# Token rows of the second expert stage: picked on chip by one-hot products in place of gathers from DRAM

## The chip, the cores and the metric

The kernel runs on one core of a Trainium2 chip. The metric is the time of one launch on the device, in microseconds (us); lower is better. TensorE is called PE (its weight loads PEld), VectorE DVE, ScalarE ACT, GpSimd POOL and SyncE SP, as in the profile.

## What is computed

The program is a stack of layers over 256 token rows of 1024 numbers, all in float32: a first block (two mixers, two feed-forward layers) and a second block of two layers, each ending in a mixture of experts. This is the mixture, cut to what matters here:

```
g_idx = top 1 of 4 groups;  top_i = top 2 of the 8 experts in it;  gate = softmax(top_v) * g_val
order = argsort(e_flat); row_tok = the token of each sorted slot; xb = x_pad[row_tok]
def expert_block(xblk, e): return (silu(xblk @ w1[e]) * (xblk @ w3[e])) @ w2[e]
out[row_tok] += yb * row_gate
```

There are 32 experts; w1 and w3 are 1024 x 512 and w2 is 512 x 1024, so one expert's weights are three matrices of 2 MB. The first expert stage routes 512 rows (256 tokens and 256 context rows), the second 256. A token goes to two experts, so in the second stage an expert gets 16 rows on average.

## The kernel before, in words

The class `Experts` holds both stages; `nt` is the number of 128-row token tiles, 4 in the first stage and 2 in the second. The text below is about the second (`nt == 2`).

The experts are taken in 16 pairs. A pair has 128 slots, 64 (`CAP`) for each of its two experts; a token's slot in its expert is its rank among the tokens that chose the expert. Rows past 64 go to an overflow loop that runs only if there are any; in this profile it does not run. The normed and modulated token rows stand in SBUF in `XM`, two tiles of 128 rows (columns 0 to 2047 of the arena Z), and ACT's copies of them are also written to DRAM, to `xm_dram`, by POOL (L2478).

Pair 0 gets its rows by a one-hot product (`pe_first`, L2042): DVE builds `SEL`, for each token and slot a 1 where the token's place equals the slot, and PE multiplies `XM` with it, which gives the rows already turned (the model dimension on the partitions). Every other pair c gets them by an indirect DMA that POOL issues (L2483): slot r reads the row of `xm_dram` that `LIST[r, c]` names, and a slot without a token has an index past the bound and reads nothing. It lands in `XG[:, c % 2]`. `XG` is the same memory as `XM[:, 0:2]`, and `c % 2` is one of two buffers: so the first gather waits until pair 0 is turned, and gather c for `turn1.{c-2}`. PE then turns the 128 x 1024 rows with 8 transposes (`pe_turn`, L2031), and ACT and DVE copy the two banks to `XT[c % 2]` (L2230, L2289).

The order on PE in a pair c is written out: w1 product (`pe_hidden` q=0, L2058, 32 matmuls), w3 product (q=1, 32 more), `pe_turn(c + 1)`, the combine of pair c-1 (L2091: 4 matmuls that spread the outputs back over tokens, which DVE adds to X, L2411), 4 transposes of the hidden rows (L2068), w2 product (L2078, 32 matmuls). For c = 0 the turn of pair 1 stands at the end of the pair. On DVE a pair is: product of the two hidden halves (L2416), copy of the turned rows (L2289), 4 adds, `PICK` (L2428), two products with the gates (L2404), which wait for the w2 product.

The weights of a pair are 6 loads of 2 MB (L1995), 96 in all, from SP in order; load n goes to slot n % 8 of eight 2 MB areas and waits until the product that used load n-8 is done. Loads 6c and 6c+1 are w1 of pair c, 6c+2 and 6c+3 w3, 6c+4 and 6c+5 w2. Nothing but these slots orders the loads against PE.

Of the kernel before, what the change touches and what calls it, by code (L numbers as in the profile page):

```python
# [22 lines left out]
P = 128  # L23
# [154 lines left out]
def build_program(nc, a, out, table, PARAM_AT, stop=None):  # L178

    ctx = ExitStack()  # L180
    with ctx:
# [36 lines left out]
        def upto(who, key):  # L218
            return table.get((who, key), 1)
# [1698 lines left out]
        class Experts:  # L1918
            def __init__(self, layer, nt, before, following):
                self.l, self.nt, self.before, self.following = layer, nt, before, following  # L1920
                L = f"moe{layer}"
                self.L = L
                s = lambda n: sem(f"{L}_{n}")
                self.w_loaded = [s(f"weights{i}_loaded") for i in range(MSLOTS)]
                self.xm_written = s("inputs_written")
                self.rows_in = [s(f"rows_in{b}") for b in range(2)]
                self.units = [(t, n) for g in range(nt // 2) for n in range(2) for t in (2 * g, 2 * g + 1)]
                self.free = "yx" if nt == 2 else "yc"
                self.selected = s("over_selection_steps")
                self.picked, self.xa = s("over_rows_picked"), s("over_rows_copied")  # L1930
                self.t1, self.m1, self.t2, self.m2 = s("over_rows_turned"), s("over_hidden_ready"), s("over_hidden_turned"), s("over_block_ready")
                self.xt, self.sl, self.y = s("over_rows_t_copied"), s("over_silu_done"), s("over_block_copied")
                self.h, self.g = s("over_hidden_copied"), s("over_gated_done")
                self.slots_turned, self.slots_of = s("over_slots_turned"), s("over_slots_copied")
                self.block, self.made, self.added = s("over_outputs_copied"), s("over_sums_ready"), s("over_sums_added")
                self.o_loaded, self.o_rows = s("over_loaded"), s("over_inputs_loaded")
                self.w = [a[f"w{j}_2"][layer] for j in (1, 3, 2)]
                self.rb = RB[:, 0:2 * nt].rearrange("p (t k) -> p t k", t=nt)

                self.owners = sorted((n for n in before_moe[layer]), key=[n for n, _ in stream].index)  # L1940
                self.slots = [slots[slot_of[n]] for n in self.owners[:4]] + [Z[:, 4096:8192], Z[:, 8192:12288], slots[slot_of[self.owners[4]]], HTF]
                self.o_slots = [self.slots[i] for i in (4, 5, 7)]
                self.OXM = self.slots[6].rearrange("p (t n) -> p t n", t=4)
                self.OS = Z[:, 0:CAP * nt].rearrange("p (t r) -> p t r", t=nt)
                self.ohit = Z[:, 256:256 + 2 * CAP * nt].rearrange("p (t k r) -> p t k r", t=nt, k=2)
                R = XSF[:, 0:1024]
                self.LG = R[:, 0:36 * nt].rearrange("p (t n) -> p t n", t=nt)
                self.OH = R[:, 144:144 + 64 * nt].rearrange("p (t k e) -> p t k e", t=nt, k=2)
                self.CT = R[:, 400:400 + 32 * (nt + 1)].rearrange("p (t e) -> p t e", t=nt + 1)
                self.CNT, self.EX, self.END, self.STA = [R[:, 656 + 32 * i:688 + 32 * i] for i in range(4)]  # L1950
                self.OHW = YW[1][:, 0:64 * nt].rearrange("p (t k e) -> p t k e", t=nt, k=2)
                self.FIRST = R[:, 560:560 + 2 * nt].rearrange("p (t h) -> p t h", t=nt)
                self.SEL = XSF[:, 1280:1280 + 2 * CAP * nt].rearrange("p (t h r) -> p t h r", t=nt, h=2)
                self.TM = SM[:, 256:256 + 64 * nt].rearrange("p (t k e) -> p t k e", t=nt, k=2)
                self.M8 = R[:, 784:784 + 8 * nt].rearrange("p (t n) -> p t n", t=nt)
                self.IF = R[:, 816:816 + 8 * nt].rearrange("p (t n) -> p t n", t=nt)
                self.OHT = XSF[:, 1024:1024 + 64 * nt].rearrange("p (t k e) -> p t k e", t=nt, k=2)
                self.HR = YW[0][:, 0:2 * CAP * nt].rearrange("p (t k r) -> p t k r", t=nt, k=2)
                q = lambda i, n: SM[:, 512 + 16 * i:512 + 16 * i + n]
                self.gm, self.gv, self.g0, self.tmp = [q(i, nt) for i in range(4)]  # L1960
                self.GO = q(4, 4 * nt).rearrange("p (t g) -> p t g", t=nt)
                self.G2 = q(5, 4 * nt).rearrange("p (t g) -> p t g", t=nt)
                self.GW = q(6, 2 * nt).rearrange("p (t k) -> p t k", t=nt)
                self.rk, self.qq, self.st, self.sl_, self.ov = [q(i, 2 * nt).rearrange("p (t k) -> p t k", t=nt) for i in range(7, 12)]
                self.EC = SM[0:1, 256:768].rearrange("p (j e) -> p j e", j=16)
                self.EO = R[0:1, 848:868]
# [30 lines left out]
            def sp(self, sp, tiles):  # L1997
# [8 lines left out]
                sp.wait_ge(sems["pe"], upto("pe", f"{self.L}.out1.{PAIRS - 1}"))  # L2006
                n = sp.value_load(OVF[0:1, 16:17], min_val=0, max_val=15)
                with sp.If(n > 0):
                    sp.dma_start(self.OXM[:, 0:self.nt, :], xm_dram[0:P * self.nt, :].rearrange("(t p) d -> p t d", p=P)).then_inc(self.o_rows, 16)
                    with sp.Fori(0, n) as j:  # L2010
                        sp.wait_ge(self.y, j + 1)
                        e = sp.value_load(OVF[0:1, bass.ds(j, 1)], min_val=0, max_val=NE - 1)
                        for k in range(3):
                            src = self.w[k][bass.ds(e, 1)].rearrange("a (p k) n -> p (a k n)", p=P)
                            sp.dma_start(self.o_slots[k], src).then_inc(self.o_loaded, 16)
# [6 lines left out]

            def pe_turn(self, te, c):
                pe, p, L, b = te.eng, te.p, self.L, c % 2
                pe.wait_ge(self.rows_in[b], 16 * (c // 2) + 16 * b)
                if c >= 1:
                    pe.wait_ge(sems["act"], upto("act", f"{L}.xt0.{c - 1}"))
                    pe.wait_ge(sems["dve"], upto("dve", f"{L}.xt1.{c - 1}"))
                for hf in range(2):
                    for j in range(4):  # L2030
                        m = pe.transpose(PS[:, hf, P * j:P * j + P], XG[:, b, 512 * hf + P * j:512 * hf + P * j + P], ident)  # L2031
                    p.step(m, f"{L}.turn{hf}.{c}")


# [252 lines left out]
            def dve_xt(self, dv, p, c):  # L2287
                dv.wait_ge(sems["pe"], upto("pe", f"{self.L}.turn1.{c}"))
                p.step(dv.tensor_copy(XT[c % 2][1], PS[:, 1, :].rearrange("p (j r) -> p j r", j=4)), f"{self.L}.xt1.{c}")  # L2289

            def dve(self, dv, p):
                L, nt, l = self.L, self.nt, self.l

                def do(instr, *key):
                    p.step(instr, *key)
                    p.settle()
# [34 lines left out]
                for t in range(nt):  # L2331
# [14 lines left out]
                do(dv.scalar_tensor_tensor(out=self.FIRST, in0=rank[:, :, 0:2], scalar=1.0, in1=self.CT[:, 0:nt, 0:2], op0=ALU.add, op1=ALU.mult))  # L2346
                p.step(dv.tensor_tensor(self.SEL, four(self.FIRST, CAP), cst("iota")[:, 1:CAP + 1].unsqueeze(1).unsqueeze(1).to_broadcast([P, nt, 2, CAP]),
                                        ALU.is_equal), f"{L}.sel")
                do(dv.tensor_tensor(self.TM, self.OH, per_choice(rank.unsqueeze(2)), ALU.mult))
                do(dv.tensor_reduce(self.rk, self.TM, AXX, ALU.add))  # L2350
                p.step(dv.tensor_tensor(self.HR, four(self.rk, CAP), row_of(cst("iota"), CAP), ALU.is_equal), f"{L}.hot")
                p.step(dv.tensor_copy(self.CNT, PS[:, 4, 32 * nt:32 * nt + 32]), f"{L}.rk")
                self.dve_xt(dv, p, 0)
                dv.wait_ge(sems["pe"], upto("pe", f"{L}.lists"))
                do(dv.tensor_scalar(LIST[:, 0:PAIRS], PS[:, 5, 0:PAIRS], float(NO_TOKEN), None, ALU.add), f"{L}.list")
                for t in range(nt):
                    p.step(dv.tensor_scalar(TOKEN_IN[:, :, t], PS[:, 5, 0:PAIRS], float(NO_TOKEN - P * t), None, ALU.add))
# [55 lines left out]
                for c in range(PAIRS):  # L2413
# [11 lines left out]
                    else:  # L2425
                        for i in range(2 * nt):
                            add(c - 1, i)
                    p.step(dv.tensor_tensor(PICK[:, 0:nt, :], cst("iota").unsqueeze(1).to_broadcast([P, nt, P]),  # L2428
                                            TOKEN_IN[:, c, 0:nt].unsqueeze(2).to_broadcast([P, nt, P]), ALU.is_equal), f"{L}.pick.{c}")
                    if c == 1:  # L2430
                        n_over = dv.value_load(OVF[0:1, 16:17], min_val=0, max_val=15)
                    for n in range(2):
# [3 lines left out]
                    if late:  # L2436
                        self.dve_xt(dv, p, 1)
                with dv.If(n_over > 0):
                    with dv.Fori(0, n_over) as j:
                        dv.wait_ge(self.selected, 6 * j + 1)  # L2440
                        dv.tensor_tensor(self.ohit, four(self.rb, CAP), row_of(cst("iota"), CAP), ALU.is_equal).then_inc(self.selected, 1)
# [31 lines left out]
            def pool(self, po):  # L2473
# [4 lines left out]
                    po.dma_start(xm_dram[P * t:P * t + P, :], XM[:, t, :]).then_inc(self.xm_written, 16)  # L2478
                po.wait_ge(sems["dve"], upto("dve", f"{L}.list"))
                po.wait_ge(self.xm_written, 16 * self.nt)  # L2480
                for c in range(1, PAIRS):
                    po.wait_ge(sems["pe"], upto("pe", f"{L}.turn1.{max(c - 2, 0)}"))
                    po.indirect_dma_start(XG[:, c % 2, :], None, xm_dram[:, :], bass.IndirectOffsetOnAxis(ap=LIST[:, c:c + 1], axis=0),  # L2483
                                          bounds_check=4 * P - 1, oob_is_err=False).then_inc(self.rows_in[c % 2], 16)
# [160 lines left out]
```

## Time and profile before

| | |
|---|---|
| median of 3 runs | 2274.24 us (2269.87 to 2276.2) |
| the profiled execution, its own time | 2264.46 us |
| its span | 2262.6 us |
| PE busy | 2153.8 us (95%) |
| DVE, ACT, POOL busy | 882.4 (39%), 314.9 (14%), 46.6 us (2%) |
| moved by DMA | 612.00 MB, mean 270 GB/s |
| mean granted PE clock | 0.984 of full speed |

The span runs from the first to the last instruction of the core. Busy shares are means over the whole span. The second expert stage fills the last fifth: PE starts pair 0 at 1788.7 us, the last weights arrive near 2241 us, and the last add is at 2258.3 us. A granted clock of 1.00 is 2.4 GHz and 0.50 is 1.2 GHz.

### The profile page before, as it was taken

To read this page: it belongs to the slowest core of one execution; us is meant where nothing else is said; L and a number is where in the kernel's file an instruction comes from. 1 tells how busy PE (TensorE), PEld (TensorE's weight loads), DVE (VectorE), ACT (ScalarE), POOL (GpSimd) and SP (SyncE) were. 2 spreads that over 40 slices of the span, in tenths; PEclk is the share of its full clock that TensorE was granted. 3 is DMA by queue.
4 is the path that set the end of the run, shared out by engine and by line. 5 is a ranking of instruction groups with operands and counts; after the bars stand their busy time and mean duration, and the time that the engine had idled before them with its cause. 6 is when DMAs were issued, how large, how long until landed. Compare 5 with 4: busy or idle time off the path is not lost.

```text
span 2262.6 us, 21849 instructions
## 1 busy us (share of the span) xinstructions
PE 2153.8 (95%) x8991; PEld 1129.6 (50%) x8991; DVE 882.4 (39%) x1623; ACT 314.9 (14%) x686; POOL 46.6 (2%) x62
## 2 busy tenths in 40 slices
PE   7999999998999999999899999999899899989898
PEld 4557766455577764444633333333345543333333
DVE  3336665326365654022432333323575422121122
ACT  2221001215310003000100000000134100000000
POOL 0000000000000000000100000000000000000000
PEclk9999999998999999999899999999999899999999
DMA  9347766350276675121899999999320899999995
GB/s 356 119 149 260 260 238 232 124 186 34 81 261 226 243 269 186 40 74 38 349 424 418 413 411 418 414 413 394 130 76 1 350 427 425 427 428 426 427 427 243
DMA packets 142532, 612.00 MB, mean 270 GB/s; under 512 B 15320, under 2 KB 66200, under 8 KB 117728
## 3 DMA queue, kind: packets, MB, share of 16 engines
q1 hardware_dynamic: 135328, 596.07, 66.7%
q0 software_dynamic: 7008, 14.40, 1.8%
q8 instruction: 74, 1.21, 0.2%
q14 instruction: 26, 0.21, 0.0%
q10 hardware_dynamic: 96, 0.10, 0.0%
HBM read 616.07 MB, written 4.33 MB: 274 GB/s over the span
## 4 chain that ended last, share of the span: by engine, by line
PE 91%; ACT 3%; DVE 3%; issue 2%; DMA 1%; SPq 0%; ACTq 0%; DVEq 0%
PE psum L2058 19%; PE psum L494 14%; PE psum L981 13%; PE psum L2078 10%; PE psum L2091 8%; PE psum L956 6%; PE psum L1559 4%; PE psum L534 3%; PE psum L2031 1%; PE psum L969 1%; PE psum L607 1%; PE psum L2068 1%; PE psum L480 1%; ACT consts L2253 1%; PE psum L1695 1%
## 5 line engine op out<-in xcount | busy, mean ns | idle before, releaser
L981 PE MATMUL psum<-normed_t,ring 128*128 128x256 f32 x1408 | 305.5, 379 | 0.0
L981 PEld LDWEIGHTS psum<-normed_t,ring 128*128 128x128 f32 x1408 | 267.5, 190 | 40.6 <-issue 4.3
L494 PE MATMUL psum<-ring,normed_t 128*128 128x512 f32 (+1 forms) x672 | 267.0, 557 | 9.9 <-DVE small L447 2.5
L886 DVE SCALAR_TENSOR_TENSOR arena<-ring,silu_c,arena 128x1024 f32<-128x1024 f32 x168 | 204.5, 1278 | 0.0
L494 PEld LDWEIGHTS psum<-ring,normed_t 128*128 128x128 f32 x672 | 124.3, 200 | 142.5 <-issue 140.9
L2078 PE MATMUL psum<-ring,consts 128*64 128x512 f32 x640 | 169.8, 594 | 21.5 <-ACT consts L2253 19.7
L2416 DVE TENSOR_TENSOR scaled<-scaled,psum 128x512 f32<-128x512 f32 x32 | 22.0, 687 | 426.8 <-PE psum L2058 426.8
L2091 PE MATMUL psum<-consts 128*128 128x512 f32 x384 | 186.1, 606 | 1.1 <-DVE small L447 0.2
L2058 PE MATMUL psum<-ring,arena 128*64 128x512 f32 x640 | 173.4, 609 | 9.7 <-issue 9.2
L2058 PE MATMUL psum<-ring,consts 128*64 128x512 f32 x640 | 168.4, 593 | 6.8 <-issue 6.8
L2411 DVE TENSOR_TENSOR resid<-resid,psum 128x512 f32<-128x512 f32 x192 | 131.8, 687 | 48.2 <-PE psum L2091 48.2
L2404 DVE SCALAR_TENSOR_TENSOR consts<-psum,consts,rows_bcast 128x512 f32<-128x512 f32 x96 | 69.3, 749 | 208.0 <-PE psum L2078 208.0
L956 PE MATMUL psum<-ring,arena 128*128 128x512 f32 x288 | 126.3, 596 | 0.0
L2058 PEld LDWEIGHTS psum<-ring,arena 128*64 128x64 f32 x640 | 62.3, 141 | 113.0 <-issue 113.0
L2078 PEld LDWEIGHTS psum<-ring,consts 128*64 128x64 f32 x640 | 59.3, 137 | 111.4 <-issue 111.4
L2091 PEld LDWEIGHTS psum<-consts 128*128 128x128 f32 x384 | 59.9, 188 | 107.0 <-DVE resid L2411 86.9
L2058 PEld LDWEIGHTS psum<-ring,consts 128*64 128x64 f32 x640 | 59.1, 137 | 107.9 <-issue 107.3
L956 PEld LDWEIGHTS psum<-ring,arena 128*128 128x128 f32 x288 | 53.9, 190 | 72.5 <-issue 72.0
L1559 PE MATMUL psum<-normed_t,ring 128*128 128x512 f32 x192 | 82.6, 592 | 0.0
L2248 ACT ACTIVATE scaled<-psum 128x512 f32<-128x512 f32 x32 | 19.1, 597 | 439.0 <-PE psum L2058 439.0
L1041 DVE SCALAR_TENSOR_TENSOR arena<-psum,params,arena 128x255 f32<-128x255 f32 x44 | 21.2, 481 | 150.7 <-ACT arena L1012 150.7
L1012 ACT ACTIVATE arena<-psum,params 128x256 f32<-128x256 f32 x44 | 24.9, 566 | 381.1 <-PE psum L981 381.1
(398 smaller groups left out, 2217.0 us busy)
## 6 DMA issues: line engine op xcount, KB each, us to landing
ring<-in_w SPq DMA_DIRECT2D x120, 2048.0 KB, 18.0
arena<-in_w SPq DMA_DIRECT2D x48, 2048.0 KB, 19.6
ring<-in_w_mod SPq DMA_DIRECT2D x24, 2048.0 KB, 8.1
normed_t<-in_w SPq DMA_DIRECT2D x24, 2048.0 KB, 21.0
ring<-in_ffn_w_up SPq DMA_DIRECT2D x44, 1024.0 KB, 9.4
ring<-in_ffn_w_down SPq DMA_DIRECT2D x10, 2048.0 KB, 9.4
ring<-in_ab_w_in SPq DMA_DIRECT2D x6, 2048.0 KB, 17.3
ring<-in_ple_w_gate SPq DMA_DIRECT2D x4, 2048.0 KB, 9.5
```

The costliest lines, as they stand in the source:

```text
L494: m = te.eng.matmul(PS[:, bank, 0:n], src[:, k0 + k, P * t:P * t + P], w[:, k, :], start=(k == 0), stop=(k == kc - 1))
L534: m = pe.matmul(PS[:, bank, :], HT[:, k, P * t:P * t + P], w[:, k, :], start=(k == 0), stop=(k == KC - 1))
L886: ins = dv.scalar_tensor_tensor(out=acc, in0=w, scalar=sc, in1=acc, op0=ALU.mult, op1=ALU.add)
L956: m = pe.matmul(PS[:, 4 + 2 * n + t, :], GT[:, c, P * t:P * t + P], w[:, cc, 512 * n:512 * n + 512], start=(c == 0), stop=(c == FC - 1))
L981: m = pe.matmul(PS[:, b, 256 * hf:256 * hf + 256], w[:, hf, k, P * cc:P * cc + P], HT[:, k, 0:T], start=(k == 0), stop=(k == KC - 1))
L1012: p.step(ac.activation(AC[:, c % 4, :], PS[:, c % 3, 0:256], ACT.Identity, bias=f_cb[i][:, c:c + 1], scale=f_cw[i][2][:, c:c + 1]), f"ffn{ ...
L1559: m = pe.matmul(PS[:, b0 + c, :], w[:, k, P * c:P * c + P], HT[:, k, :], start=(k == 0), stop=(k == KC - 1))
L2058: m = pe.matmul(PS[64 * h:64 * h + 64, 2 + q, :], XT[c % 2][k // 4][:, k % 4, 64 * h:64 * h + 64], w[h][:, k, :], start=k == 0, stop=k == ...
L2078: m = pe.matmul(PS[64 * h:64 * h + 64, 6 + n, :], HGT[:, j, 64 * h:64 * h + 64], w[h][:, j, 512 * n:512 * n + 512], start=j == 0, stop=j == 3)
L2091: m = pe.matmul(PS[:, 4 + i % 2, :], PICK[:, t, :], YW[t // 2][:, 512 * n:512 * n + 512], start=True, stop=True)
L2404: p.step(dv.scalar_tensor_tensor(out=YW[kind][:, cols], in0=PS[:, 6 + n, :], scalar=SLOT_GATE[:, c:c + 1], in1=GB[:, kind, cols], op0=ALU. ...
L2411: p.step(dv.tensor_tensor(xr, xr, PS[:, 4 + i % 2, :], ALU.add), f"{L}.add{i}.{c}", *keys)
```

## The change

For `nt == 2` the gathers are not issued. DVE keeps a table `PLACE` of each token's slot in each of the 32 experts (0 where the token did not choose it), and for each pair builds `SELS[c % 2]`, the one-hot matrix of its two experts, two pairs ahead. `pe_turn` multiplies `XM` with it, as pair 0 did, in place of the transposes. `XM` is then never overwritten. `SELS` and `PLACE` lie in a part of the arena that the second stage does not use. The rows are still written to `xm_dram`, for the overflow; the waits for that write are added there. The first stage (`nt == 4`) is as before.

```diff
@@ Experts.__init__
+                self.picks = nt == 2
+                self.PLACE = Z[:, 2560:2624].rearrange("p (t e) -> p t e", t=2)
+                self.SELS = [Z[:, o:o + 256].rearrange("p (t h r) -> p t h r", t=2, h=2) for o in (2048, 2304)]
@@ sp, in the overflow (and the same in dve)
+                    sp.wait_ge(self.xm_written, 16 * self.nt)
@@ pe_turn
-                pe.wait_ge(self.rows_in[b], 16 * (c // 2) + 16 * b)
+                if self.picks:
+                    pe.wait_ge(sems["dve"], upto("dve", f"{L}.sel.{c}"))
+                else:
+                    pe.wait_ge(self.rows_in[b], 16 * (c // 2) + 16 * b)
...
                 for hf in range(2):
                     for j in range(4):
-                        m = pe.transpose(PS[:, hf, P * j:P * j + P], XG[:, b, 512 * hf + P * j:512 * hf + P * j + P], ident)
+                        cols = slice(512 * hf + P * j, 512 * hf + P * j + P)
+                        if self.picks:
+                            for t in range(2):
+                                m = pe.matmul(PS[:, hf, P * j:P * j + P], XM[:, t, cols], self.SELS[b][:, t].rearrange("p h r -> p (h r)"),
+                                              start=t == 0, stop=t == 1)
+                        else:
+                            m = pe.transpose(PS[:, hf, P * j:P * j + P], XG[:, b, cols], ident)
@@ new
+            def dve_sel(self, dv, p, c):
+                if c > 2:
+                    dv.wait_ge(sems["pe"], upto("pe", f"{self.L}.turn1.{c - 2}"))
+                p.step(dv.tensor_tensor(self.SELS[c % 2], self.PLACE[:, :, 2 * c:2 * c + 2].unsqueeze(3).to_broadcast([P, 2, 2, CAP]),
+                                        cst("iota")[:, 1:CAP + 1].unsqueeze(1).unsqueeze(1).to_broadcast([P, 2, 2, CAP]), ALU.is_equal),
+                       f"{self.L}.sel.{c}")
@@ dve, routing: after SEL
+                if self.picks:
+                    p.step(dv.scalar_tensor_tensor(out=self.PLACE, in0=rank, scalar=1.0, in1=self.CT[:, 0:nt, :], op0=ALU.add, op1=ALU.mult))
@@ dve, routing: before LIST
+                if self.picks:
+                    self.dve_sel(dv, p, 1)
+                    self.dve_sel(dv, p, 2)
@@ dve, in each pair after PICK
+                    if self.picks and 1 <= c < PAIRS - 2:
+                        self.dve_sel(dv, p, c + 2)
@@ pool
-                for c in range(1, PAIRS):
+                for c in range(1, 1 if self.picks else PAIRS):
```

## Rows read from the trace of the kernel before

**Rows 1.** Second expert stage by stretches: us, each engine busy, PEclk, DMA share, GB/s
```profile
1790.00:2262.00 472.00, 429.38 (x1860) 171.71 (x1856) 100.36 (x173) 29.77 (x51) 14.95 (x15) 0.98 0.96 405
```
**Rows 2.** DMA queues from 1800 to 2235 us: packets, MB, share of 16 engines
```profile
q1 hardware_dynamic: 12557, 182.87, 98.9%
q0 software_dynamic: 2160, 1.97, 1.3%
```
**Rows 3.** Chain that ended last, 1740 us to the end: start us, us, what
```profile
1840.82 13.73 PE psum L2058 x64
...
1867.97 13.73 PE psum L2058 x64
...
1902.51 7.09 PE psum L2058 x32
...
1932.56 8.78 PE psum L2058 x32
...
2022.63 7.09 PE psum L2058 x32
2029.71 1.02 PE psum L2031 x8
...
2043.13 6.87 PE psum L2058 x32
2050.00 2.65 issue
2052.65 8.51 PE psum L2058 x32
...
2114.25 8.43 PE psum L2058 x32
...
2174.27 8.78 PE psum L2058 x32
...
2203.64 7.09 PE psum L2058 x32
...
2231.01 1.98 issue
2232.99 8.78 PE psum L2058 x32
2241.78 1.92 PE psum L2091 x4
```
**Rows 4.** Waits from 1790 us on: who, for whom, us in total, times, longest
```profile
PE psum L2058 <- issue: 23.3, 13, 2.7
```
**Rows 5.** PE timeline, a turn in this stage: start us, us, instructions
```profile
1827.33 1.09 PE L2031 MATMUL psum<-consts,arena 128*128 128x128 f32 x8
1828.26 1.88 PE L2091 MATMUL psum<-consts 128*128 128x512 f32 x4
```
**Rows 6.** PE timeline, the one-hot product of pair 0 in the first expert stage
```profile
1099.94 7.38 PE L2042 MATMUL psum<-scaled,arena 128*128 128x128 f32 x64 [1.07 <-DVE scaled L2347]
1107.25 0.94 PE L2157 MATMUL psum<-scaled,consts 128*64 128x16 f32 x26
```
**Rows 7.** Groups from 1780 us on: busy us, mean ns, idle before and releaser
```profile
L2404 DVE SCALAR_TENSOR_TENSOR consts<-psum,consts,rows_bcast 128x512 f32<-128x512 f32 x32 | 24.1, 752 | 111.6 <-PE psum L2078 111.6
L2428 DVE TENSOR_TENSOR consts<-consts 128x256 f32<-128x256 f32 x16 | 6.7, 420 | 0.0
```
**Rows 8.** DMA queue of the gathers in one pair, 2052.65 to 2082.67 us
```profile
q0 software_dynamic: 144, 0.11, 1.1%
```
**Rows 9.** Stretches as the weight stream ends, and as another load ends at 1609 us
```profile
2230.00:2242.00 12.00, 10.02 (x39) 3.58 (x36) 0.18 (x1) 0.60 (x1) 0.00 (x0) 0.86 0.49 208
2230.00:2231.00 1.00, 1.00 (x6) 0.13 (x2) 0.00 (x0) 0.00 (x0) 0.00 (x0) 1.00 0.96 410
2240.00:2241.00 1.00, 1.00 (x8) 0.38 (x5) 0.00 (x0) 0.00 (x0) 0.00 (x0) 1.00 0.12 49
1608.00:1609.00 1.00, 0.79 (x3) 0.30 (x2) 0.96 (x4) 0.00 (x0) 0.00 (x0) 1.00 1.02 389
1609.00:1610.00 1.00, 0.64 (x3) 0.24 (x3) 1.00 (x3) 0.00 (x0) 0.00 (x0) 1.00 0.23 84
```

More of the change, by code:

```diff
@@ L2438, in dve @@
                 with dv.If(n_over > 0):
+                    dv.wait_ge(self.xm_written, 16 * nt)
                     with dv.Fori(0, n_over) as j:
```

## The prediction

> **What bounds the kernel now.** Over the whole span PE is 95% busy, and the chain of waits is nearly all PE. For this change that is the wrong view, so I read the second expert stage alone. The busy time by stretches says that there the DMA engines are 96% busy at 405 GB/s on average [rows 1], and between 1800 and 2235 us nothing is free: the weight queue has 98.9% of the 16 engines and POOL's queue 1.3% more [rows 2]. The chain of waits then shows when that binds. Early pairs run at PE's pace: the w1 product starts at 1840.82 and the next at 1867.97, 27.15 us apart. From 1902.51 on, the chain has pieces called "issue" in front of the w3 product (L2058), as the 2.65 us before 2052.65 [rows 3]. Such a piece is a wait that the profile can't name; here it is the wait for the second w3 load of the pair, n = 6c + 3, since the w1 and w2 products that need the loads on either side start late enough. There are 13 of them, 23.3 us in all [rows 4]. The w3 products of pairs 4 and 15 start at 1902.51 and 2232.99: 330.48 us for 11 pairs, 30.04 us a pair, against 27.15 of PE's own work. So PE is ahead, the weight stream is the bound from pair 4 on, and the stream ends the kernel: when load 93 lands (2232.99), PE has the last w3 product, the combine, w2 and the last combine left, and that tail is fixed.
>
> After some of these waits the w3 product takes longer than 7.09 us: 8.78, 8.51, 8.43, 8.78 and, in the last pair, 8.78 [rows 3]. In the last one the granted clock is 0.86 over 2230 to 2242 us [rows 9]: part of it ran at 1.2 GHz after the idle. The four before the last sum to 1.69 + 1.42 + 1.34 + 1.69 = 6.14 us, which is wait in another form.
>
> **Part 1: what PE gets more.** A turn is 8 transposes now. From the start of one (1827.33) to the start of the combine (1828.26) are 0.93 us, 116 ns each [rows 5]. It becomes 16 matmuls of 128 x 128 with 128 columns, accumulated in pairs. The trace has just this form in `pe_first` of the first stage, at full clock: 64 of them start in 1107.25 - 1099.94 = 7.31 us, 114 ns each [rows 6]. 16 x 114 = 1.83 us, so a turn costs 0.90 us more, 0.92 with the transposes' own price; 15 turns make 13.8 us. I take 0.92: the upper end is a turn at the low clock, twice 1.83 less 0.93, +2.7 us, the lower end nothing, if matmuls of two tiles overlapped as transposes don't. The copies by ACT and DVE behind the turn, and the combine with its adds, shift with it.
>
> All but one turn stand behind a w3 product and ahead of the next wait for weights, so this work falls into waits that PE has anyway, as long as there are enough. The stock is the 23.3 us of waits and the 6.14 of slow products, 29.4 us up to the start of the last w3 product. Without them PE would start it at 2232.99 - 29.4 = 2203.5; with 13.8 more, at 2217.4. What is left of the cover is 15.6 us before the stream moves at all.
>
> A rule that speaks against the change is in the Trainium skill, page FP8 and Floating Point Precision, section TensorE Precision Notes: a true float32 product takes four passes through the array. The row disagrees with what it would cost: 128 columns four times at 2.4 GHz would be 213 ns, and [rows 6] has 114, no more than a transpose. By the rule 16 x 213 ns less 0.93 would be 2.48 us a turn; the sum goes by the row.
>
> **Part 2: what DVE gets more.** One `SELS` a pair, of the form of PICK: 128 x 256, 420 ns [rows 7]. It stands between PICK and the products with the gates, and these wait for the w2 product: 111.6 us of idle before 32 of them, 3.5 us each [rows 7]. So 0.42 us is hidden eight times over; without that cover it would delay the next w2 product's bank and cost up to 0.42 x 13 = 5.5 us. `PLACE` and the first two `SELS` (some 1.1 us) lie in the routing; PE is by then in the one-hot product and the 13.8 us of the first two hidden products, and DVE is next needed after those. PE's new wait for `sel.{c}` was served a pair earlier: nothing. The waits for `xm_written` stand in an overflow that does not run: nothing.
>
> **Part 3: what the DMA engines lose.** This is where the time is. 15 gathers go. POOL's queue takes 1.3% of 435 us, 5.7 us of each engine on the mean [rows 2]; small, since slots without a token read nothing (0.11 MB in one pair, not the 0.52 MB of 128 rows) [rows 8]. This is the least that the stream can gain, 0.38 us a pair.
>
> But a load is there only when the last of its 16 engines is done, and the engines are not equally late. Pairs that still have a gather ahead of their loads are 30.02 us apart (2022.63 to 2052.65); after the last gather the spacing is 29.37 and 29.35 (2174.27, 2203.64, 2232.99) [rows 3]. That is 0.66 us a gather, where the mean share of such a pair is 1.1% of 30.02, 0.33 us [rows 8]. And the end of the stream shows it: another load on this core stops within a microsecond (share 1.02, then 0.23), while the weight stream fades from 0.96 at 2230 to 0.12 at 2240 [rows 9]. Some engines are ten microseconds ahead of others, and the last one sets when load 93 is complete.
>
> The Trainium skill gives a reason (DMA: Bandwidth & Descriptors, The descriptor swizzle): an engine owns fixed partitions, the first owning 0 to 3 and 32 to 35. Used slots are the first 16 or so of each 64, so half of the engines would carry all rows, twice the mean. The 0.66 against 0.33 agrees, and with a reason beside the rows I give the case where only the mean is saved a smaller chance than the two spacings alone would leave it.
>
> How early is load 93 then? Two ways:
> - By spacing: 15 x 0.66 = 9.9 us, it lands at 2223.1.
> - By the end of the stream: over the 12 us from 2230 the mean share is 0.49, so the mean engine has 5.9 us left and ends at 2235.9. Less 5.7 for the gathers is 2230.2, for all engines alike if they are level. Load 93 is two loads before the end, 2 x 29.36 / 6 = 9.8 us: 2220.4.
> I take the middle, 2221.7, 11.3 us earlier. PE is ready at 2217.4, so the stream still sets the end, by 4.3 us: PE has waits left in the last three or four pairs only, of some 1.3 us each (29.36 less 28.07 a pair).
>
> **Sum.** The waits left are shorter than the 1.98 us that preceded the last slow product, so I count on full clock there: 7.09, not 8.78. From the end of that product to the end of the span are 2262.6 - 2241.8 = 20.8 us, unchanged (out.15 starts 5.5 us behind the product, 2234.3, and needs load 95, in by 2231.5). New span 2221.7 + 7.1 + 20.8 = 2249.6, which is 13.0 less. The profiled execution's own time 2264.46 becomes 2251.5. The median of the runs shown is 9.8 us above that execution; I take the difference over to it: 2274.24 - 13.0 = 2261.2.
>
> **Does the stream starve?** Loads wait for slots that PE now frees later. In steady state a load lands some 27 us after its issue, five to six loads queued. The longest stretch in which PE frees nothing is from a w3 product to the w2 product, 14 us with the new turn, under three loads. I see no gap.
>
> **The rivals.**
> - *PE becomes the bound* (0.13). The stream gains more than I think (level engines, faster than 29.36 a pair); then the end is PE's: 2217.4 + 27.9 = 2245.3, 17.3 us less, median 2256.9. For it: only 4.3 us lie between. Against: both of my ways end above.
> - *Only the mean is saved* (0.17). If engines are unequal for another reason, the stream gains 5.7 us, PE still waits some 2 us in the last pair and its product stays slow: median 2268.5. For it: two spacings are few. Against: the fade of ten microseconds.
> - *The freed engine time is not used* (0.07). The rate is set by the memory and not by the engines, and gathers of 2 MB in 185 cost nothing: 2 to 3 us less or nothing, median 2273. Against: 30.02 against 29.36.
> - *The product costs what four passes cost* (0.07, slower). The place is the turn, and it decides from (29.4 / 15 + 0.93) / 16 = 181 ns a matmul on, where the added work is more than the waits. At the 213 ns of the rule named above: 15 x 2.48 = 37.2 us, PE starts the last w3 product at 2240.7, span 2268.6, median 2280. For it: in the second stage the one-hot product of pair 0 ran partly at the low clock. Against: [rows 6], and PE never rests long around the turns.
> My forecast has 0.56.
>
> **How the numbers follow.** What a measurement of this kernel can tell from no change is 0.3%, 6.8 us. Faster by more than that: the forecast (nearly all of its 0.56), PE bound 0.13, a third of the mean-only case, less something for runs that scatter by 6 us: 0.71. Within: the rest of the mean-only case, the unused time: 0.21. Slower: 0.08. The range reaches from PE's bound with 3 us of scatter to the mean-only case with 2: 2253 to 2271.
>
> **What would show it.** Right: L2031 x 16 in 1.85 us; w3 products 29.4 us apart only in the last pairs, 28.1 before; "issue" ahead of L2058 down from 23.3 to some 5 us; first such wait after 2130 us; the DMA share at the stream's end falling from 1 to under 0.3 within 2 us, with the last load in near 2230; full clock in the last pair. Wrong: a spacing of 30 us that stays without gathers, a fade that stays ten microseconds long, turns above 2.9 us, or a wait of PE for `sel`.

## The result

The change makes the kernel slower: 2279.77 us median against 2271.6 us (18 runs each), 8.2 us more. The ratio on record, 1.0029 (95% interval 1.002 to 1.0037), is 6.6 us. The forecast was 13 us faster.

The two profiled executions are 15.3 us apart in span (2262.6 and 2277.9), but 8.9 of them lie ahead of the stage: before starts pair 0 at 1788.7 and after at 1797.6 us. The experiments below, with or without gathers, start it at 1793 to 1798 us, except e10, whose edit lengthens the first stage too. So the 8.9 us are hardly the change's: the profiled execution of before was a short one (2264.46 us against its median 2271.6). Everything below is therefore told from the stage alone, from the start of the first w1 product to the start of the last add: 469.6 us before (1788.74 to 2258.29), 476.0 us after (1797.60 to 2273.62). These 6.4 us are 0.28% of the whole, the ratio's size.

The chain of waits after, in the same stretch as [rows 3] (start us, us, what; L2071 is the w1 and w3 product, L2041 the turn, L2104 the combine, L2091 the w2 product):

```profile
1797.60 13.80 PE psum L2071 x64
...
1820.84 3.77 PE psum L2041 x32
1824.61 13.88 PE psum L2071 x64
...
1854.65 13.73 PE psum L2071 x64
1868.38 3.77 PE psum L2041 x32
1872.15 1.72 PE psum L2104 x4
1873.89 1.97 PE psum L2104 x4
...
1877.47 7.09 PE psum L2091 x32
1884.56 13.73 PE psum L2071 x64
...
2232.71 1.96 PE psum L2104 x4
2234.68 0.73 PE psum L2081 x4
...
2236.29 7.09 PE psum L2091 x32
...
2273.62 0.69 DVE resid L2436
```

Two things are to be seen. The w1 and w3 products are never split: no "issue" stands in front of either any more, where before there were 13 [rows 4] (12 in front of a w3 product and one, at 2103.17 us, in front of a w1 product). And a turn takes 3.77 us where the prediction had 1.85: it is 32 instructions, for 16 products in the code. The w1 product of one pair and the next are 1884.56 - 1854.65 = 29.91 us apart, and 29.90 or 29.91 from pair 2 to the end: PE never waits for weights, so this is the pace of PE's own chain.

The whole stage after (us, each engine busy, PEclk, DMA share, GB/s), and the DMA queues from 1800 to 2235 us, beside [rows 1] and [rows 2]:

```profile
1797.00:2277.00 480.00, 461.64 (x2241) 213.32 (x2240) 107.02 (x196) 29.75 (x51) 0.00 (x0) 1.00 0.94 395
```
```profile
q1 hardware_dynamic: 12518, 182.31, 99.9%
q0 software_dynamic: 124, 0.44, 0.3%
```

PE is at full clock all the time and busy 96% of it. The gathers are gone, and yet the weight queue moved no more in the same 435 us: 182.31 MB against 182.87. The share of 99.9% does not say that the stream is the bound; e5 below tests that.

### The profile page after: what moved, and what is told of

It reads as the page before. It is cut to its first block, busy times and chain, and to the rows that moved or that the text cites. A ratio compares the mean times of both kernels' runs of the same rounds, so it can differ in the third digit from the quotient of the medians.

```text
span 2277.9 us, 22556 instructions
## 1 busy us (share of the span) xinstructions
PE 2190.4 (96%) x9351; PEld 1172.8 (51%) x9351; DVE 887.7 (39%) x1639; ACT 314.7 (14%) x686; POOL 31.7 (1%) x47
## 4 chain that ended last, share of the span: by engine, by line
PE 91%; DVE 3%; ACT 2%; DMA 2%; issue 1%; SPq 0%; DVEq 0%; POOL 0%; ACTq 0%; POOLq 0%
PE psum L2071 19%; PE psum L494 14%; PE psum L981 13%; PE psum L2091 10%; PE psum L2104 8%; PE psum L956 6%; PE psum L1559 4%; PE psum L534 2%; PE psum L2041 2%; PE psum L969 1%; PE psum L607 1%; PE psum L480 1%; PE psum L2044 1%; PE psum L1695 1%; DMA expert_inputs<-arena 1%
## 5 line engine op out<-in xcount | busy, mean ns | idle before, releaser
L2091 PE MATMUL psum<-ring,consts 128*64 128x512 f32 x640 | 169.8, 594 | 21.3 <-ACT consts L2266 10.7
L2104 PE MATMUL psum<-consts 128*128 128x512 f32 x384 | 186.1, 606 | 1.2 <-DVE small L447 0.2
L2071 PE MATMUL psum<-ring,arena 128*64 128x512 f32 x640 | 168.0, 592 | 0.0
L2071 PE MATMUL psum<-ring,consts 128*64 128x512 f32 x640 | 167.7, 592 | 0.0
L2091 PEld LDWEIGHTS psum<-ring,consts 128*64 128x64 f32 x640 | 59.4, 137 | 111.1 <-issue 111.1
L2104 PEld LDWEIGHTS psum<-consts 128*128 128x128 f32 x384 | 60.0, 189 | 107.0 <-DVE resid L2436 86.9
L2071 PEld LDWEIGHTS psum<-ring,arena 128*64 128x64 f32 x640 | 61.1, 137 | 99.4 <-issue 99.2
L2071 PEld LDWEIGHTS psum<-ring,consts 128*64 128x64 f32 x640 | 59.9, 137 | 98.9 <-issue 98.4
## 6 DMA issues: line engine op xcount, KB each, us to landing
ring<-in_w SPq DMA_DIRECT2D x120, 2048.0 KB, 13.4
```

The costliest lines, as they stand in the source:

```text
L2071: m = pe.matmul(PS[64 * h:64 * h + 64, 2 + q, :], XT[c % 2][k // 4][:, k % 4, 64 * h:64 * h + 64], w[h][:, k, :], start=k == 0, stop=k == ...
L2091: m = pe.matmul(PS[64 * h:64 * h + 64, 6 + n, :], HGT[:, j, 64 * h:64 * h + 64], w[h][:, j, 512 * n:512 * n + 512], start=j == 0, stop=j == 3)
L2104: m = pe.matmul(PS[:, 4 + i % 2, :], PICK[:, t, :], YW[t // 2][:, 512 * n:512 * n + 512], start=True, stop=True)
```

## The experiments

The ratio is to the kernel before, on the same chip; the stage is from one profiled execution of each. e1 and e2 leave token rows out: they are probes and no usable kernels.

| kernel | ratio, 95% interval | stage, us |
|---|---|---|
| before | 1 | 469.6 |
| the change | 1.0029, 1.002 to 1.0037 | 476.0 |
| e1 half the pick | 0.996, 0.9945 to 0.9975 | 457.9 |
| e2 turn only | 0.9959, 0.9944 to 0.9973 | 457.9 |
| e3 spread slots | 0.9986, 0.9976 to 0.9997 | 465.7 |
| e4 first nine picked | 0.9985, 0.9974 to 0.9996 | 465.8 |
| e5 picks and gathers | 1.0027, 1.0015 to 1.0038 | 476.1 |
| e6 rows, then turn | 1.0094, 1.0079 to 1.0108 | 491.9 |
| e7 nine interleaved | 0.9969, 0.9958 to 0.9981 | 462.3 |
| e8 one bfloat16 part | 0.9957, 0.9943 to 0.9972 | 458.6 |
| e9 two bfloat16 parts | 0.996, 0.9947 to 0.9973 | 458.2 |
| e10 double turn | 1.0047, 1.0031 to 1.0063 | 467.6 |

**e1, half the pick.** Was only the price of the product wrong, or the stream as well?

```diff
-  for t in range(2): m = pe.matmul(PS[...], XM[:, t, cols], SELS[b][:, t], start=t == 0, stop=t == 1)
+  m = pe.matmul(PS[...], XM[:, 0, cols], SELS[b][:, 0], start=True, stop=True)
```


> As the changed kernel, but the pick of pairs 1 to 15 multiplies only the first of the two token tiles: 8 products a turn in place of 16 (the rows of tokens 128 to 255 are left out there). Theory A, the stream was forecast rightly and only the price of a product was wrong (3.77 us a turn, not 1.83): a turn takes 1.9 us, PE's own pace is 28.0 us a pair, and this is the kernel that was forecast: the last w3 product starts some 11 us earlier than before relative to the first product of the stage, the stage (first w1 product to last add, 469.6 us before, 476.0 after) takes 455 to 459 us, the median falls by 11 to 14 us, and first waits of PE for weights come only late. Theory B, without gathers the stream gains only their mean share: 464 us, median -6. Theory C, it gains nothing: 468 us or more, median 0 to -2.

The chain of waits of this kernel, late in the stage (L2070 is the hidden product, L2040 the turn), and its stretches as the stream ends:

```profile
1835.43 1.98 PE psum L2040 x16
...
2200.15 1.02 issue
2201.16 7.09 PE psum L2070 x32
...
2229.50 1.01 issue
2230.50 7.09 PE psum L2070 x32
```
```profile
2234.00:2235.00 1.00, 1.00 (x8) 0.48 (x6) 0.00 (x0) 0.00 (x0) 0.00 (x0) 1.00 0.92 393
2238.00:2239.00 1.00, 1.00 (x4) 0.38 (x2) 0.63 (x2) 0.00 (x0) 0.00 (x0) 1.00 0.35 147
2239.00:2240.00 1.00, 0.99 (x3) 0.30 (x2) 0.83 (x2) 0.00 (x0) 0.00 (x0) 1.00 0.04 16
```

Theory A, nearly to the number: waits of 1.0 us in the last pairs, w3 products 29.34 us apart, full clock, stage 457.9. The last w3 product starts 2230.50 - 1796.26 = 434.2 us into the stage, against 2232.99 - 1788.74 = 444.3 before: the stream is 10.0 us earlier, the 9.9 of the spacing. The median is 10.7 us lower (9.1 by the ratio), just under the 11 to 14 expected; the profiled stage gains 11.7.

**e2, turn only.** The stream alone.

```diff
-  for t in range(2): m = pe.matmul(PS[...], XM[:, t, cols], SELS[b][:, t], ...)
+  m = pe.transpose(PS[...], XM[:, b, cols], ident)
```


> As the changed kernel, no gathers, but the turns are the 8 transposes of before, of the token tiles themselves (so the rows of the slots are left out). PE's own pace is 27.15 us as before, so only the stream differs from before. Theory A: w3 products 29.4 us apart where PE waits, the last one 10 to 12.5 us earlier within the stage, the end of the stream sharp (from full to under 0.3 within 2 us); stage 457 to 460 us, median -10 to -13. Theory B: spacing 29.6 to 29.7, stage 464, median -6. Theory C: spacing 30.0, stage 469, median 0.

The last w3 product starts 2231.56 - 1797.23 = 434.3 us into the stage, the same as in e1 although PE has 0.96 us less to do per turn. So in both the stream sets the end. The end of the stream is sharper, though not as sharp as I wrote: it fades over 4 us, not 10. The stage is 457.9 us, as theory A had it; the median is 9.7 us lower (9.3 by the ratio), just short of the 10 to 13 expected.

**e3, spread slots.** The gathers stay; only where the used slots lie is changed.

```diff
+  for k, place in enumerate((SPREAD0, SPREAD1)):     # slot 32i + 8j + e on partition 32i + 4e + j
+      dv.tensor_copy(place.rearrange("p (i e j) -> p i e j", i=2, e=8), iota[:, k:k + 64].rearrange("p (i j e) -> p i e j", i=2, j=4))
-  SEL = (place == iota[1:65]);   HR = (rank == iota[0:64])
+  SEL = (place == SPREAD1);      HR = (rank == SPREAD0)
```


> As the kernel before, with all its gathers, but in the second stage a token's slot is moved to another partition, so that slots 0 to 7 of an expert lie 4 partitions apart, 8 to 15 beside them, and so on: the rows that a gather does read are spread over all partitions. Nothing else changes (two small copies on DVE more). Theory A, the cost of a gather is set by the engines that carry its rows: a gather costs 0.3 to 0.4 us and not 0.66, spacing 29.7, the stream ends sharply, median -4 to -6. Theory B or C, the mean share or nothing counts: spacing 30.0 and the same long fade, median 0.

Two w3 products that follow each other in this kernel's chain of waits:

```profile
2000.23 7.09 PE psum L2060 x32
...
2029.95 7.09 PE psum L2060 x32
```

The most frequent spacing of the w3 products fell from 30.02 to 29.7 us, 29.36 without a gather ahead: a gather costs 0.37 us, not 0.66. The last one starts 3.8 us earlier in the stage. The ratio is 0.9986, 3 us, somewhat less than the 4 to 6 expected. The stream's end is sharp, though it still has all its gathers (from full to under a third in two to three microseconds, where [rows 9] have a fade of ten):

```profile
2243.00:2244.00 1.00, 1.00 (x6) 0.33 (x4) 0.00 (x0) 0.00 (x0) 0.00 (x0) 0.75 1.00 426
2245.00:2246.00 1.00, 1.00 (x8) 0.41 (x6) 0.00 (x0) 0.00 (x0) 0.00 (x0) 1.00 0.27 115
```

So the same bytes cost less, and the long fade goes, when their rows lie on more partitions. That each engine writes fixed partitions is the Trainium skill's reason (DMA: Bandwidth & Descriptors, The descriptor swizzle), and the edit was made by it; the page describes it for a plain transfer to 128 partitions. The views read here give only the mean of the 16 engines, so the trace shows the effect and not which engine was late.

**e4 and e7, nine pairs picked.** First the first nine, then nine spread over the stage, with the gathers of the others landing in a dead part of X.

```diff
e4  +  picked = c <= 9
e7  +  picked = c in (1, 3, 5, 7, 8, 9, 11, 13, 15);   XG = X[:, 2:4]
```


> Pairs 1 to 9 by the one-hot product, pairs 10 to 15 by gathers and transposes. Theory A: PE's own work in the stage is 435.4 + 2.3 + 8 x 2.75 = 459.7 us, the stream has 9 gathers less and ends the stage at 462 to 463.5 us, so the two nearly meet; median -6 to -7.5, faster than both kernels. Theory B: the stream gains 9 x 0.38 = 3.4 us, stage 466, median -3.5. Theory C: 468 to 469 us, median 0.

e4 came out at theory B's numbers: stage 465.8 us, ratio 0.9985, the last w3 product 3.7 us earlier in the stage and not 5.9. But B's reason, that a gather costs only its mean share, is at odds with e1 and e2, where 15 gathers were worth 10.0 us. Another reason fits: in pairs 1 to 9 PE takes 29.9 us and never waits for weights; it can free slots only at that pace, and a stream that could do a pair in 29.36 has nowhere to put its lead. The time of a load from issue to landing bears it out, here of the loads into the ring from 1800 to 2235 us in e4 and after the change (count, size, median us). A load is a sixth of a pair, some 4.9 us of the stream, so by my estimate the 27.0 us before are 5.5 loads in line, the 22.4 of e1 4.6, and the 13.4 after the change 2.7:

```profile
ring<-in_w SPq DMA_DIRECT2D x55, 2048.0 KB, 16.1
```
```profile
ring<-in_w SPq DMA_DIRECT2D x55, 2048.0 KB, 13.4
```

If that is the reason, the order of the picked pairs must matter:

> Nine pairs picked as in the run with pairs 1 to 9, but spread over the stage (1, 3, 5, 7, 8, 9, 11, 13, 15), the other six by gathers. Theory A, in the run with the first nine the weight stream was held at PE's 29.90 us a pair, since all eight weight slots were full, and lost 9 x 0.5 us: here PE's pace is below the stream's in the mean, the stream gains its 9 x 0.66 = 5.9 us, stage 464 to 465 us, last w3 product 438.3 us after the first w1 product, median -5 to -6. Theory B, a removed gather is worth only some 0.4 us: stage 466.5 as before, median -2 to -3.

It does: the same number of picks and gathers, the last w3 product starts 2235.69 - 1796.78 = 438.9 us into the stage (e4: 440.5), stage 462.3, ratio 0.9969; stage and ratio are a little better than theory A, the w3 product is 0.6 us later. The loads from 1830 to 2090 us, in e4 and then in e7, waited 14.5 and 20.1 us:

```profile
ring<-in_w SPq DMA_DIRECT2D x33, 2048.0 KB, 14.5
```
```profile
ring<-in_w SPq DMA_DIRECT2D x35, 2048.0 KB, 20.1
```

Two limits of this test: the gathers of e7 also land elsewhere than those of e4, and in e7 PE waits for weights only twice, 2.3 us in all, and not in the last pair. The stage of e7 is thus little more than PE's own 459.7 us (the sum in the expectation of e4) and these waits; it shows that the stream was no later, not that it gained just 5.9 us.

**e5, picks and gathers.** Does the stream have any part in the changed kernel's time?

```diff
-  for c in range(1, 1 if self.picks else PAIRS):
+  for c in range(1, PAIRS):          # into X[:, 2, :], which nobody reads; each waits for the one before
```


> The changed kernel with its 15 gathers back as well; they land in a dead area and nobody reads them. Theory A, PE sets the pace of the changed kernel (29.90 us a pair), and the stream with gathers (30.02) would be no slower than its first lead covers: stage 476 to 478 us, median as the changed kernel, 7 to 9 us over the kernel before. Theory B, the stream still has a part in the changed kernel's time: stage 5 to 10 us longer than 476.7.

No. Stage 476.1 us with 15 gathers, 476.0 without, and no wait of PE for weights in either. The changed kernel is bound by PE.

**e6, rows, then turn.** The one-hot matrix stationary, rows moving, then 8 transposes.

```diff
+  for hf in range(2):
+      for t in range(2): m = pe.matmul(PS[:, hf, :], SELS[c % 2][:, t], XM[:, t, 512 * hf:512 * hf + 512], start=t == 0, stop=t == 1)
```


> No gathers. The one-hot matrix is the stationary operand and the token rows move, 512 columns at a time: 4 products a pair give the rows of the slots, ACT and DVE copy them to SBUF, and the 8 transposes of before turn them. By the combine's rows (8 instructions of 512 columns, 215 ns each for 4 products) the pick is 8 x 0.215 = 1.72 us in place of the 2.75 that the changed kernel adds. Theory A: PE's pace is 28.9 us a pair, under the stream's 29.36; PE's own work in the stage is 435.4 + 15 x 1.75 = 461.7, so the stage is 461 to 463 us, median -7 to -9 against the kernel before. Theory B, the copies between pick and transposes hold PE: stage above 468.

Wrong, by a row's count once more. The chain of waits of this kernel (L2053 is the pick):

```profile
1812.01 3.63 PE psum L2053 x8
```

4 products are 8 instructions of 454 ns. A row "PE psum L2091 x4" of 1.72 us in the combine before is 4 instructions, which is two products; I had spread its time over 8 instructions and four products. PE's pace is 30.94 us, the stage 491.9. That is past theory B's 468, but not by its reason: the chain has the hidden product right behind the pick, and no wait for the copies.

**e8 and e9, bfloat16.** If a float32 product is two instructions, a product of another type should take fewer.

```diff
e8  +  XMB = bf16(XM);  pe.matmul(PS[...], XMB[:, t, cols], SELB[b][:, t], ...)                 # 2 products per bank quarter
e9  +  XHI = bf16(XM);  XLO = bf16(XM - XHI)   # once, on ACT and DVE
e9  +  for k in range(4): pe.matmul(PS[...], (XHI, XLO)[k % 2][:, k // 2, cols], SELB[b][:, k // 2], start=k == 0, stop=k == 3)
```


> The changed kernel with the token rows and the one-hot matrix in bfloat16 for the picks of pairs 1 to 15 (the rows picked are rounded to bfloat16); 16 products a turn as in the changed kernel. Theory A, a float32 product is issued as two instructions of some 118 ns and a bfloat16 one as a single one: the turn is 16 instructions and takes 1.0 to 1.9 us, the stream is the bound again, stage 457 to 460, median -9 to -12. Theory B, the count of products is what costs: turn 3.8 us, stage 476.

> The picks of pairs 1 to 15 with the token rows as a sum of two bfloat16 parts, high and low (made once, by ACT and DVE), so the rows come out to some 16 bits in place of 8: 32 bfloat16 products a turn. At the 62 ns of the run with one bfloat16 part a turn is 2.0 us, PE's pace 28.15 us a pair, below the stream's 29.36. Theory A, the stream sets the end: stage 458 to 459 us, median -9 to -11 against the kernel before, as with one part. Theory B, the two extra passes over the rows on DVE (some 2 us each way) delay the start of the stage's pairs: stage 461 or more.

Chains of waits, e8 and then e9 (L2046 is the turn in both, L2076 the hidden product):

```profile
1969.27 1.00 PE psum L2046 x16
```
```profile
2060.82 1.89 PE psum L2046 x32
...
2082.02 1.23 issue
2083.25 7.09 PE psum L2076 x32
```

16 products are now 16 instructions, 62 ns each. In e9 the 32 of them take 1.89 us, half of the float32 pick, PE is ahead of the stream again, and the kernel comes near what was forecast of the change: stage 458.2, 11.4 us less than before, ratio 0.996. It beats both kernels, and loses some of float32's last bits in the picked rows; e8 rounds them to 8 bits. e7 is the fastest of those that keep the rows as they are. The two passes of DVE over the rows cost nothing that the stage shows.

**e10, double turn.** Is the cover that the prediction counted really free?

```diff
-  for j in range(4):
+  for j in (0, 1, 2, 3) * 2:
```


> The kernel before, each turn's 8 transposes done twice in both expert stages (same result). In the second stage that is 0.93 us more of PE's work in 15 pairs, 14 us, under the cover of 32 us of waits. Theory A: there nothing changes, stage 469 to 471 us with waits of PE down from 23.3 to some 12 us; the first stage has no such cover and pays 15 x 0.93 = 14 us, so the median is +14. Theory B, the waits are not free cover: stage up by 5 us or more.

The wait ahead of the hidden products in this kernel, beside [rows 4], and a turn in its chain:

```profile
PE psum L2058 <- issue: 15.6, 8, 3.0
```
```profile
1849.66 1.90 PE psum L2031 x16
```

Free it is: a double turn takes 1.90 us and not 1.02, so PE has 15 x 0.88 = 13.2 us more, and the stage is no longer (467.6), with 8 waits and 15.6 us where there were 13 and 23.3. The waits shrank by 7.7 us only (some 12 left were expected); most of the rest came out of the slow w3 products, five before and one now. The median is 10.3 us up: with 2.0 us won in this stage the first one pays some 12, where PE sets the pace (expected 14).

## Why the prediction was wrong

- *What bounds the kernel now.* Right. The weight stream from pair 4 on; e10 shows the waits to be free cover for 13.2 us of work, e2 shows that the stream moves the end. One of the 13 waits was in front of a w1 product, not a w3 product.
- *Part 1, the price of a product.* This is the step that failed: "64 of them start in 7.31 us, 114 ns each. 16 x 114 = 1.83 us". The x64 of [rows 6] are instructions. `pe_first` has 2 x 4 x 4 = 32 products there; each float32 product is issued as two instructions, and a transpose as one. The turn measured 3.77 us, so 2.75 us more than the transposes' 1.02 and not 0.92. With that PE and not the stream sets the pace, 29.91 us a pair against the stream's 29.36: the stage is 6.4 us longer where 13.0 less were forecast. With the price halved (e1), the rest of the forecast came nearly true. The same slip stands in the text on the kernel, which calls the w1 product 32 matmuls where `pe_hidden` has 8 x 2 calls (w3 and w2 likewise); the combine, 4 calls and twice "x4" in the chain, would have shown it.
- *The rule weighed there.* The Trainium skill (FP8 and Floating Point Precision, TensorE Precision Notes) gives a true float32 product four passes; 213 ns at 128 columns was my estimate from it. I held the row against it; read rightly the traces agree: two instructions of 118 ns, 236 a product, and 62 in bfloat16 (e8), a ratio of 3.8. The rival that carried it got 0.07; it said 2.48 us more a turn and 6.0 us more in all, and 2.75 and, in the stage, 6.4 were measured. It also named where it decides, 181 ns a product. That its 2280 us met the median of 2279.77 is part luck: its base was the 2274.24 of three runs, and the median of 18 is 2271.6.
- *The cover.* 29.4 us were counted. It was 34: besides the waits (23.3) and slow products (6.1, and 1.7 in the last pair), the w1 and w3 products of a pair take 6.87 + 7.09 us when a wait splits them and 13.73 when none does, 13 x 0.23 = 3.0. The added work is 14 x 2.75 + 2.29 (the first turn, whose copy was exposed before) = 40.8. 469.6 - 34.1 + 40.8 = 476.3; measured 476.0.
- *Part 2, DVE.* Right: one-hot matrices of 419 ns, w2 still starts 1.6 us behind the combine as before, PE waits for no `sel`. The profile names DVE's one-hot line (L2307) as releaser of the w2 product in 13 pairs, but a pair without it has the same gap (2234.67 to 2236.29) as one with it (1875.86 to 1877.47).
- *Part 3, the stream.* Right in kind, and in size by the way of the spacing: 9.9 us forecast, 10.0 and 9.9 measured (e1, e2). The way by the end of the stream (12.6) was too high, since a stream without gathers still fades over some 4 us; the mean of both, 11.3, was 1.3 too much. That unlevel engines are the cause is supported by e3, where the same rows on other partitions cost 0.37 us a gather in place of 0.66 and the long fade is gone.
- *Starving.* "I see no gap" holds only while PE's pace is below the stream's. With the true price it was not, and e4 against e7 shows what that costs, 3.5 us of the stage.
- Not settled: single pairs that are 1 to 2 us late in several runs (31.58 us in before from 2082.67, 31.28 in e3), and why the medians of e1 and e2 gain 1 to 3 us less than their stages.

## What to carry to other kernels

A row's count is of instructions: hold it against the calls in the code before dividing, for each type and kind, and let a documented rule that disagrees by a factor of two send you back to that count. Where a fixed stream is the bound, other engines have a stock of cover that can be added up from the chain (waits, slow pieces, splits), and here 13.2 us of work under a stock of 34 were free, while 40.8 cost the difference, 6.4 us. An engine slower than the stream also throttles it, through the buffers that it frees late. A busy share near 1 didn't tell the stream that was the bound (98.9%) from the throttled one (99.9%); the time from issue to landing did (27.0 and 13.4 us).

## What the runs showed of the hardware

- At full clock, 128 x 128 stationary and 128 columns: a float32 transpose is one instruction of 116 to 128 ns, a float32 product two of 118 ns (32 in 3.77 us), a bfloat16 product one of 62 ns (16 in 1.00 us). With 512 columns a float32 product is two of 454 ns (8 in 3.63 us).
- An indirect gather of some 30 used rows of 4 KB delayed the 2 MB loads beside it by 0.66 us with its rows in neighbouring partitions, and by 0.37 us with the same rows spread (e3).
- The same DMA share of 1.00 at 416 GB/s in the changed kernel, where weight slots come free late, and at 426 before, where they don't: the stretch from 1850 to 1900 us after and then before (us, each engine busy, PEclk, DMA share, GB/s).

```profile
1850.00:1900.00 50.00, 49.08 (x242) 22.52 (x238) 8.50 (x13) 2.39 (x4) 0.00 (x0) 1.00 1.00 416
```
```profile
1850.00:1900.00 50.00, 48.17 (x214) 19.94 (x212) 11.94 (x18) 2.99 (x5) 1.98 (x2) 1.00 1.00 426
```
